# Scan readout in four column groups with four transfers a round, its products in banks of their own, rotary products one round later, nine lags

## The chip, the cores and the metric

The kernel runs on one core of one Trainium2 chip. The metric is the device time of one execution in microseconds (us): the kernel before takes 1859.64 us, the median of three runs (1855.35 to 1863.19). The engines are TensorE (PE in the rows; PEld is its weight load), VectorE (DVE), ScalarE (ACT), GpSimd (POOL) and SyncE (SP); ACT and SP also issue transfers (ACTq, SPq).

## What is computed

Two layers. Each projects its input (256 context and 256 latent tokens, width 1024) to a bidirectional state-space scan (S5), a grouped-query attention with rotary positions and a neighbourhood attention, gates and merges the three, and runs a mixture of 16 experts. The change is in the scan's readout and in the rotary step beside it:

```python
def apply_axial_rope(x, cos, sin):
    ...
    out = jnp.stack([x1 * cs - x2 * sn, x2 * cs + x1 * sn], axis=-2)
...
def s5_bidirectional(u_ctx, u_lat, lam_re, lam_im, log_dt, b_re, b_im, c_re, c_im, d_skip, need_ctx):
    ...
    def scan_direction(seq, d):
        lam_bar = jnp.exp(lam * dt)
        b_bar = ((lam_bar - 1.0) / lam)[..., None] * lax.complex(b_re[d].astype(f32), b_im[d].astype(f32))
        bu = jnp.einsum('blgh,gph->blgp', ug.astype(jnp.complex64), b_bar)
        _, states = lax.associative_scan(_recurrence_combine, (a, bu), axis=1)
    ...
    def readout(states, d):
        y = jnp.einsum('blgp,ghp->blgh', states, cm).real
    ...
    y_lat = (readout(st_f[:, n_ctx:], 0) + readout(st_b[:, :n_lat], 1)
             + dsk * u_lat.astype(f32)).astype(u_lat.dtype)
```

There are 32 groups of 16 channels with 64 complex states each, in two directions.

## The kernel before

**The scan in blocks of eight tokens.** The 512 tokens are 64 blocks of 8 steps. What a block takes from earlier blocks comes through its carried state `st`; what it takes from its own tokens comes through a 128 x 128 matrix per group (8 steps x 16 channels on either side), built from the products of `cre`, `cim` with powers of the transition (`pws`), here called lags. `cp` holds those products: 128 partitions (64 states of the forward direction, 64 of the backward), `NPOS` = 10 lag positions x 16 channels, for 4 groups, real and imaginary, two buffers.

**The loop around the change.** After the scan of the block states, each layer runs `for q in range(NQ + 1)`: 8 rounds of 4 groups and one round to finish. The loop is written once for each engine. In the order of the instructions, round q holds:

- TensorE: **z(q)**, 16 products that contract the 64 states of one direction (`bb`, 16 columns, stationary) with eight of the lags in `cp` (128 columns): the block matrix's entries, forward and backward in two PSUM banks, on partitions 0 to 15. **y(q-1)**, 24 products (128 x 64): `tm` by the input `ug`, and `cp` by the carried states `st`, into two banks. Then the four small products that turn a row of modulation weights into columns (`mc`), the sum of squares of a head's queries or keys (`qk_ms`, rounds 0 to 4), eight products of an input projection (rounds 0 to 4), eight column-tiled products of modulation weights (`mr`, 32 columns x 512), and in rounds 0 to 4 the **rotary product** of the same q, which waits for VectorE's normalised queries (`qnorm_done`). In rounds 5 to 8 of layer 0 an `mr` and an `mc` of the next layer come in as well. All of them are recorded at the helper's line L618; one fp32 product leaves two records.
- ScalarE: copies the forward bank of z into `zs` (L1132), waits for VectorE's part (`zd_done`), issues four of the eight transfers `zs` to `tm` (L1285), then the root of `qk_ms` (L1142) and the copies of projections and of modulation rows (`mrow`).
- VectorE: carries the block states (L1565 to L1568), copies and adds the backward bank of z and the skip weights into `zs` (`readout_rows`, L1528 to L1532), adds up y (L1815, L1817), the modulation block (L1737), for the last two rounds half of the `cp` products (`readout_part`, L1551 to L1553), the reciprocal and scaling of queries and keys (L1831, L1832), and the three rotary operations (L1837 to L1840).
- GpSimd: builds `cp` for a later round, six operations over 640 elements (L1992 to L2000), three in the rounds it shares with VectorE. Its buffer is one of two, so round q's starts when y(q-2) is complete.
- SyncE: the ring of weights from HBM (L535, 1 MB each) and the other four transfers to `tm` (L570), later the attention's bias (L540), which waits until the last y has been taken.

**Transfers to `tm`.** `zs` holds 16 rows and, for each group, 15 lags x 16 columns. Step j of the block matrix is a window of 128 columns that begins 16 columns further on, so one transfer for each j writes 16 partitions of `tm` for four groups.

**PSUM banks.** Nearly all products share four banks (`tile_ps`) that rotate by a list of jobs (`tile_jobs`); z and y take two each a round. A product waits until the bank it gets has been emptied. The banks `turn_ps` and `out_ps` are used elsewhere and idle in this loop.

## Time and profile before

| | us |
|---|---|
| median of three runs | 1859.64 |
| the profiled execution | 1862.84 |
| its span, first to last instruction | 1861.1 |
| TensorE busy | 1696.2 (91%) |
| VectorE / ScalarE / GpSimd busy | 704.6 / 417.7 / 302.4 |
| readout loop of layer 0, its stretch in the span | 177.3 to 314.3 |
| readout loop of layer 1 | 1241.3 to 1355.4 |

A view by stretches gives the busy time of each engine, the mean granted clock of TensorE (1.0 is its upper level, 2.4 GHz, 0.5 its lower, 1.2 GHz) and the share of time in which the transfer engines were busy. A timeline lists instructions in order of their start, with the idle time ahead of one and what ended it in square brackets. A table of waits sums up that idle time. The chain of work is followed back from the end, step by step, to what released each step.

### The profile page before, as it was taken

The numbers are of one execution on the slowest core, as the hardware profiler recorded it, in microseconds if no ns is written. First come the engines' busy times: TensorE is split into PE (matmuls) and PEld (weight loads), VectorE is DVE, ScalarE is ACT, GpSimd is POOL, SyncE is SP. The second block draws the span as 40 slices with busy tenths as digits, with TensorE's granted clock in tenths as the row PEclk, the third lists the DMA queues.
The fourth block names the chain that finished last, engine by engine and source line by source line (L and its number), as shares of the span: only waits on it lengthen the run. The fifth ranks groups of instructions, "written<-read, shape, count | busy, mean of one in ns | idle before, by whom it ended". The sixth has DMA issues, their size and how long they took to land.

```text
span 1861.1 us, 28871 instructions
## 1 busy us (share of the span) xinstructions
PE 1696.2 (91%) x11470; PEld 1028.1 (55%) x11470; DVE 704.6 (38%) x1564; ACT 417.7 (22%) x866; POOL 302.4 (16%) x263
## 2 busy tenths in 40 slices
PE   5999998889999999899988988999889999996697
PEld 2467455554444443555555556676547888453354
DVE  3678764650110112311101168596763111421123
ACT  4011212551000001322222250111144001331133
POOL 0004342870000000200000020045364000000000
PEclk9999998999999999999999988998999999998899
DMA  9410369419221153499999533125571346899991
GB/s 391 127 46 24 129 220 334 87 59 342 97 108 72 68 226 136 171 386 364 384 391 393 210 115 113 46 74 197 203 140 51 154 167 245 345 401 410 411 360 58
DMA packets 108139, 384.07 MB, mean 206 GB/s; under 512 B 42016, under 2 KB 61472, under 8 KB 68864
## 3 DMA queue, kind: packets, MB, share of 16 engines
q1 hardware_dynamic: 85872, 335.43, 48.2%
q0 software_dynamic: 4272, 30.67, 4.8%
q10 hardware_dynamic: 17888, 16.42, 3.1%
q8 instruction: 81, 1.33, 0.3%
q14 instruction: 26, 0.21, 0.0%
HBM read 363.09 MB, written 31.98 MB: 212 GB/s over the span
## 4 chain that ended last, share of the span: by engine, by line
PE 63%; DVE 12%; DMA 8%; SPq 7%; POOL 4%; issue 3%; ACT 3%; ACTq 1%; POOLq 0%; DVEq 0%
PE tile_ps L618 56%; SPq L535 6%; PE turn_ps L618 3%; DMA arena<-sorted_in 3%; POOL arena L2010 3%; DMA vn<-in_wpack 2%; PE out_ps L618 1%; DMA ring<-in_wpack 1%; PE turn_ps L939 1%; DVE arena L1873 1%; DMA arena<-in_rpb 1%; DMA x<-in_xT 1%; DVE arena L1518 1%; DVE arena L1565 1%; DVE arena L1516 0%
## 5 line engine op out<-in xcount | busy, mean ns | idle before, releaser
L618 PE MATMUL tile_ps<-h,ring 128*128 128x512 f32 (+1 forms) x1312 | 480.4, 522 | 7.1 <-ACT h L1149 5.0
L618 PEld LDWEIGHTS tile_ps<-h,ring 128*128 128x128 f32 x1312 | 255.2, 196 | 216.1 <-issue 199.6
L618 PE MATMUL tile_ps<-arena 128*32 128x256 f32 (+5 forms) x3152 | 271.7, 351 | 19.2 <-ACT arena L1374 4.9
L618 PE MATMUL tile_ps<-arena,ring 128*128 128x512 f32 (+1 forms) x704 | 235.3, 486 | 2.7 <-issue 2.7
L618 PEld LDWEIGHTS tile_ps<-arena 128*32 128x32 f32 (+4 forms) x3152 | 182.2, 140 | 77.5 <-issue 46.9
L618 PEld LDWEIGHTS tile_ps<-arena,ring 128*128 128x128 f32 x704 | 133.6, 190 | 96.6 <-issue 87.6
L2010 POOL TENSOR_SCALAR arena<-arena,smx 128x512 f32<-128x512 f32 (+1 forms) x96 | 128.5, 1358 | 64.0 <-DVE smx L1861 63.6
L618 PE MATMUL tile_ps<-ring,arena 128*32 128x256 f32 (+2 forms) x1008 | 93.9, 418 | 17.1 <-DMA ring<-in_wpack 12.4
L1347 ACT ACTIVATE arena<-tile_ps 128x512 f32<-128x512 f32 (+1 forms) x56 | 27.5, 491 | 347.3 <-PE tile_ps L618 347.3
L1894 DVE TENSOR_TENSOR arena<-tile_ps,arena 128x512 f32<-128x512 f32 (+1 forms) x32 | 17.8, 558 | 212.2 <-PE tile_ps L618 212.2
L1992 POOL TENSOR_TENSOR arena<-arena 128x640 f32<-128x640 f32 x16 | 22.1, 1380 | 353.4 <-PE tile_ps L618 353.3
L618 PEld LDWEIGHTS tile_ps<-ring,arena 128*32 128x32 f32 (+1 forms) x1008 | 49.1, 123 | 52.0 <-issue 34.1
L618 PE MATMUL tile_ps<-qn,arena 128*64 128x256 f32 (+1 forms) x272 | 65.2, 395 | 12.9 <-DMA vn<-in_wpack 12.9
L1712 DVE TENSOR_TENSOR arena<-tile_ps,arena 64x256 f32<-64x256 f32 x24 | 10.0, 417 | 175.6 <-ACT arena L1219 175.6
L1972 POOL TENSOR_SCALAR h<-h,amuls,mods 128x256 f32<-128x256 f32 x12 | 12.1, 1020 | 393.1 <-DVE h L1586 353.7
L618 PE MATMUL tile_ps<-ring,h 128*128 128x256 f32 (+1 forms) x384 | 72.0, 350 | 0.0
L1316 ACT ACTIVATE arena<-tile_ps,smx 128x512 f32<-128x512 f32 (+1 forms) x96 | 58.6, 616 | 57.9 <-DVE smx L1855 57.8
L939 PE MATMUL turn_ps<-con,arena 128*128 128x128 f32 x320 | 52.2, 288 | 19.0 <-DVE arena L1865 11.7
L618 PEld LDWEIGHTS tile_ps<-ring,h 128*128 128x128 f32 x384 | 64.2, 194 | 7.0
L618 PE MATMUL tile_ps<-qa,arena 128*64 128x256 f32 (+1 forms) x272 | 65.2, 395 | 0.0
L1855 DVE TENSOR_REDUCE smx<-tile_ps 128x1 f32<-128x512 f32 (+1 forms) x96 | 54.8, 598 | 26.4 <-PE tile_ps L618 25.1
L939 PEld LDWEIGHTS turn_ps<-con,arena 128*128 128x128 f32 x320 | 34.0, 142 | 54.8 <-issue 25.4
(316 smaller groups left out, 2274.6 us busy)
## 6 DMA issues: line engine op xcount, KB each, us to landing
ring<-in_wpack SPq DMA_DIRECT2D x176, 1024.0 KB, 7.6
arena<-in_wpack SPq DMA_DIRECT2D x64, 1024.0 KB, 16.5
h<-in_wpack SPq DMA_DIRECT2D x15, 1024.0 KB, 25.3
qa<-in_wpack SPq DMA_DIRECT2D x12, 1024.0 KB, 9.6
qn<-in_wpack SPq DMA_DIRECT2D x12, 1024.0 KB, 12.8
kn<-in_wpack SPq DMA_DIRECT2D x12, 1024.0 KB, 15.0
vn<-in_wpack SPq DMA_DIRECT2D x12, 1024.0 KB, 17.0
sorted_out<-arena ACTq DMA_DIRECT2D x44, 128.0 KB, 7.6
```

What stands on the lines that cost most here:

```text
L535: sp.dma_start(dst, src).then_inc(arrived, 16)
L618: return nc.tensor.matmul(out, lhsT, rhs, start=start, stop=stop)
L939: ins = nc.tensor.transpose(turn_ps[:, half, t * P:(t + 1) * P], probs[:, N % (LAG + 1), half, t * P:(t + 1) * P], c("ident"))
L1316: A(probs[:, N % (LAG + 1), half, 0:nk], bank((l, "sc", n, half))[:, 0:nk], ACT.Exp, bias=smx[:, 0, at:at + 1], accum_out=smx[:, 1, at:at ...
L1347: free(job, A(sig[:, n % 2, c0:], bank(job)[:, c0:], ACT.Sigmoid))
L1518: link(TT(nxt, nxt, tmp[0], ALU.add))
L1565: ins = TT(tmp[k], spread(came, 1, STEP), spread(pwb[:, k, 0:STEP, gs], 3, NB - 1), ALU.mult)
L1855: dve.tensor_reduce(smx[:, 0, at:at + 1], bank(job)[:, 0:nk], AX.X, ALU.max, negate=True).then_inc(max_done, 1)
L1873: link(TT(b, b, spread(c("far_cols"), 1, 2 * GRID_H), ALU.add))
L1894: free(job, TT(v, bank(job)[:, c0:], s, ALU.mult))
L1992: link(TT(o0, pv[0], cv[0], ALU.mult))
L2010: pool.tensor_scalar(v, v, smx[:, 2, at:at + 1], None, ALU.mult).then_inc(prob_done, 1)
```

## The change

- `NPOS` is 9 instead of 10: the forward lags are positions 0 to 7 for z and 1 to 8 for y, the backward ones 1 to 8 and 0 to 7, so both directions lie in nine positions. GpSimd's and VectorE's `cp` operations shrink from 640 to 576 elements.
- z's stationary matrix gets 32 columns (`bb_on`; the upper 16 are the next group's and their results aren't used). Group g of the round writes partitions 32g to 32g + 31 of `turn_ps`, forward in one bank and backward in another, so the products lie on eight tiles of 64 rows x 32 columns. `zs` is 128 partitions with 240 columns: the copies are 128 x 128 and 128 x 112 instead of 16 x 512 and 16 x 448.
- One transfer for each group, whose source is the overlapping windows of 16 rows (`lag_rows`), writes all 128 partitions of `tm`: four a round, two issued by SP and two by ACT, instead of eight. The order of `tm`'s rows changes from (step, channel) to (channel, step), and with it the input `ug`, `pww`, `wm` and the skip weights.
- y goes to `out_ps`. z and y have semaphores of their own (`z_full`, `z_free`, `y_full`, `y_free`) and no jobs in the rotation of `tile_ps`. Before the attention, TensorE waits for `y_free` and `z_free`, ScalarE ahead of its store of y for `y_free`.
- The rotary product of q - 1 moves into round q, behind `mc`; VectorE's three rotary operations move behind y's sum (and behind `readout_part`), in `rotated`.

```diff
-NPOS = STEP + 2
+NPOS = STEP + 1
...
-ON_SP = 4
+ON_SP = 2
...
-            names += [(l, "z", q, 0), (l, "z", q, 1)] if q < NQ else []
...
+            names += late
+            names += [(l, "rope", q - 1)] if 0 < q <= KW + 1 else []
...
-            names += [(l, "rope", q)] if q <= KW else []
...
+        def lag_rows(g):
+
+            v = zs[32 * g:32 * g + GRP, 0:P]
+            (step, n), (one, m) = v.ap
+            return bass.AP(tensor=v.tensor, offset=v.offset, ap=[[step, n], [GRP, STEP], [one, m]])
...
-                    for j in range(STEP - ON_SP, STEP):
-                        a = (STEP - 1 - j) * GRP
-                        sp.dma_start(tm[j * GRP:(j + 1) * GRP, q % 2], zs[:, :, a:a + P]).then_inc(tm_in, 16)
...
+                    for g in range(GQ - ON_SP, GQ):
+                        sp.dma_start(tm[:, q % 2, g], lag_rows(g)).then_inc(tm_in, 16)
+                sp.wait_ge(y_free, (l + 1) * NQ)
...
+                        if l * NQ + q:
+                            for n in range(2):
+                                pe.wait_ge(z_free[n], l * NQ + q)
+                        for r in range(2):
+                            for g in range(GQ):
...
+                                    ins = mm(turn_ps[32 * g:32 * g + 32, n, 0:P], bb_on[d, at_g:at_g + 32],
                                              cp[d, r, at_q, lags].rearrange("p a b -> p (a b)"), r == 0, r == 1)
...
+                    if 0 < q <= KW + 1:
+                        pe.wait_ge(qnorm_done, l * (KW + 1) + q)
+                        v = qa[:, q - 1, CTX:] if q - 1 < KW else ka[:, CTX:]
+                        product((l, "rope", q - 1), [(c("rot"), v)], bank((l, "rope", q - 1))[:, 0:LAT])
...
-                    if q <= KW:
-                        pe.wait_ge(qnorm_done, l * (KW + 1) + q + 1)
-                        v = qa[:, q, CTX:] if q < KW else ka[:, CTX:]
-                        product((l, "rope", q), [(c("rot"), v)], bank((l, "rope", q))[:, 0:LAT])
 
                 us = pairs[l]
+                for taken in (y_free, *z_free):
+                    pe.wait_ge(taken, (l + 1) * NQ)
...
-                link(CP(pww[F], pw[F, :, 0:STEP][:, :, ::-1]))
-                link(CP(pww[B], pw[B, :, 0:STEP]))
+                link(CP(pww[F], pw[F, :, 0:STEP].rearrange("p r j g -> p r g j")))
+                link(CP(pww[B], pw[B, :, 0:STEP][:, :, ::-1].rearrange("p r j g -> p r g j")))
...
+                    if 0 < q <= KW + 1:
+                        rotated(l, q - 1)
...
-                    if q >= 2:
-                        wait_full(pool, (l, "yb", q - 2))
-                        wait_full(pool, (l, "y", q - 2))
+                        pool.wait_ge(y_full, l * NQ + q - 1)
```

TensorE in rounds 0 and 1 of layer 0, before: `arena 16x128` are z's products, `arena 128x64` y's, `con,mrow` is `mc`, `qsq,con` is `qk_ms`, `h,ring` the projection, `ring,csil` is `mr`, `qa,con` the rotary product.

```order
L618 MATMUL tile_ps<-ring,csil 32x512 x8
L618 MATMUL tile_ps<-qa,con 128x256
L618 MATMUL tile_ps<-arena 16x128 x16
L618 MATMUL tile_ps<-arena 128x64 x24
L618 MATMUL tile_ps<-con,mrow 128x2 x4
L618 MATMUL tile_ps<-qsq,con 128x512
L618 MATMUL tile_ps<-h,ring 128x512 x8
L618 MATMUL tile_ps<-ring,csil 32x512 x8
L618 MATMUL tile_ps<-qa,con 128x256
```

The same place now:

```order
L623 MATMUL tile_ps<-ring,csil 32x512 x8
L623 MATMUL turn_ps<-arena 32x128 x16
L623 MATMUL out_ps<-arena 128x64 x24
L623 MATMUL tile_ps<-con,mrow 128x2 x4
L623 MATMUL tile_ps<-qa,con 128x256
L623 MATMUL tile_ps<-qsq,con 128x512
L623 MATMUL tile_ps<-h,ring 128x512 x8
L623 MATMUL tile_ps<-ring,csil 32x512 x8
```

The rotary product left the end of the round, where it stood right behind VectorE's scaling, for the middle of the next one; z and y write other banks.

VectorE in one round of layer 1, before, from the scaling of queries to the next one (L1565 to L1568 carry the states, L1528 to L1532 are `readout_rows`):

```order
L1832 SCALAR_TENSOR_TENSOR qa<-qa,qg,rstd 128x256
L1837 TENSOR_TENSOR qrt<-tile_ps,con 128x256
L1838 TENSOR_TENSOR qa<-qa,con 128x256
L1840 TENSOR_TENSOR qa<-qa,qrt 128x256
L1565 TENSOR_TENSOR arena<-arena 128x224 x2
...
L1528 COPY arena<-tile_ps 16x4x112
L1530 TENSOR_TENSOR arena<-arena,tile_ps 16x4x16
L1532 TENSOR_TENSOR arena<-arena 16x4x16
L1815 COPY arena<-tile_ps 128x256
L1817 TENSOR_TENSOR arena<-arena,tile_ps 128x256
L1737 TENSOR_TENSOR mods<-tile_ps,mis 128x8
```

The same round now:

```order
L1848 SCALAR_TENSOR_TENSOR qa<-qa,qg,rstd 128x256
L1571 TENSOR_TENSOR arena<-arena 128x224 x2
...
L1534 COPY arena<-turn_ps 128x112
L1536 TENSOR_TENSOR arena<-arena,turn_ps 128x16
L1538 TENSOR_TENSOR arena<-arena 128x16
L1830 COPY arena<-out_ps 128x256
L1831 TENSOR_TENSOR arena<-arena,out_ps 128x256
L1754 TENSOR_TENSOR mods<-tile_ps,mis 128x8
L1744 TENSOR_TENSOR qrt<-tile_ps,con 128x256
L1745 TENSOR_TENSOR qa<-qa,con 128x256
L1747 TENSOR_TENSOR qa<-qa,qrt 128x256
```

The three rotary operations moved from ahead of the states' carry to behind y's sum.

SP's transfers in the first rounds of layer 0, before and then now:

```order
L570 DMA arena<-arena 16x4x128 x4
L535 DMA ring<-in_wpack 128x2048 x4
L570 DMA arena<-arena 16x4x128 x4
L535 DMA ring<-in_wpack 128x2048
L570 DMA arena<-arena 16x4x128 x4
```

```order
L576 DMA arena<-arena 128x1x128 x2
L542 DMA ring<-in_wpack 128x2048 x4
L576 DMA arena<-arena 128x1x128 x2
L542 DMA ring<-in_wpack 128x2048
L576 DMA arena<-arena 128x1x128 x2
```

Two transfers of 128 rows stand where four of 64 rows stood; the weights' place between them is the same.

## Rows read from the trace of the kernel before

**Rows 1.** Busy time (instructions), granted clock, transfer share, GB/s, by stretches of both loops.

```profile
core 0: us, PE busy (x) PEld busy (x) DVE busy (x) ACT busy (x) POOL busy (x), PEclk, DMA share, GB/s
177.30:199.00 21.70, 19.58 (x85) 8.69 (x84) 19.51 (x46) 5.83 (x9) 0.00 (x0) 0.98 0.45 156
199.00:267.60 68.60, 67.47 (x497) 37.67 (x496) 43.88 (x76) 11.17 (x19) 33.96 (x24) 0.96 0.39 126
267.60:314.30 46.70, 41.57 (x467) 26.94 (x466) 22.87 (x59) 6.01 (x11) 8.43 (x6) 0.93 0.97 375
...
1241.30:1260.10 18.80, 18.80 (x87) 8.63 (x88) 16.19 (x44) 5.04 (x9) 0.00 (x0) 1.00 0.40 130
1260.10:1319.10 59.00, 56.42 (x497) 40.90 (x496) 38.04 (x76) 9.57 (x20) 33.87 (x24) 0.88 0.51 170
1319.10:1355.40 36.30, 29.82 (x369) 22.45 (x370) 25.84 (x53) 3.48 (x6) 9.80 (x6) 0.90 0.79 283
```

**Rows 2.** TensorE's waits in the loop of layer 0: us, times, longest.

```profile
PE tile_ps L618 <- ACT mrow L1132: 4.2, 4, 1.8
PE tile_ps L618 <- DVE qa L1832: 2.1, 1, 2.1
PE tile_ps L618 <- DVE arena L1817: 1.3, 3, 0.6
```

**Rows 3.** TensorE's waits in the loop of layer 1.

```profile
PE tile_ps L618 <- DVE arena L1553: 3.8, 1, 3.8
PE tile_ps L618 <- POOL arena L1995: 1.9, 1, 1.9
```

**Rows 4.** Timeline of TensorE, layer 1: start, duration, records.

```profile
1241.37 1.92 PE L618 MATMUL tile_ps<-arena 64*16 64x128 f32 x32
...
1264.78 1.05 PE L618 MATMUL tile_ps<-con,mrow 128*128 128x2 f32 x8
1265.70 0.68 PE L618 MATMUL tile_ps<-qsq,con 128*128 128x256 f32 x2
1266.33 5.38 PE L618 MATMUL tile_ps<-h,ring 128*128 128x256 f32 x16
1271.64 1.92 PE L618 MATMUL tile_ps<-ring,csil 128*32 128x512 f32 x16
1273.50 0.70 PE L618 MATMUL tile_ps<-qa,con 128*128 128x256 f32 x2
1274.29 4.78 PE L618 MATMUL tile_ps<-arena 64*16 64x128 f32 x80
...
1311.45 3.69 PE L618 MATMUL tile_ps<-h,ring 128*128 128x256 f32 x16 [0.57 <-DVE arena L1817]
...
1352.59 3.04 PE L618 MATMUL tile_ps<-arena 64*128 64x64 f32 x48
```

**Rows 5.** Chain of work in layer 1, rounds 1 to 2: start, duration, what.

```profile
1264.93 0.42 issue
1265.36 1.34 POOL arena L1992
...
1272.70 1.55 POOL arena L2000
...
1274.29 13.94 PE tile_ps L618 x124
```

**Rows 6.** Timeline, layer 1, two stretches: the same VectorE operation beside GpSimd and alone.

```profile
1293.21 1.33 POOL L1992 TENSOR_TENSOR arena<-arena 128x640 f32<-128x640 f32 x1 [5.01 <-PE tile_ps L618]
1293.27 1.34 DVE L1532 TENSOR_TENSOR arena<-arena 16x64 f32<-16x64 f32 x1
...
1294.54 0.41 DVE L1815 COPY arena<-tile_ps 128x256 f32<-128x256 f32 x1
...
1334.40 0.21 DVE L1532 TENSOR_TENSOR arena<-arena 16x64 f32<-16x64 f32 x1
```

**Rows 7.** ACT's twelve transfers to `tm` in rounds 5 to 7 of layer 0.

```profile
DMA to landing us min/median/max: 3.2/4.3/5.1
```

More of the change, by code:

```diff
@@ L344, in backbone @@
         into = st[:, STEP]
-        pww, a0 = cut(a0, [2, STEP, NGRP])
+        pww, a0 = cut(a0, [2, NGRP, STEP])
         pws, a0 = cut(a0, [2, NPOS, NGRP])
@@ L867, in _ @@
                             pe.wait_ge(cp_other, l * len(SHARED) + SHARED.index(q) + 1)
-                        for n in range(2):
-                            wait_bank(pe, (l, "z", q, n))
-                        for g in range(GQ):
-                            at_q = (q % 2) * GQ + g
-                            for r in range(2):
-                                for n, (d, lags) in enumerate(((lower, slice(0, STEP)), (upper, slice(2, NPOS)))):
-                                    ins = mm(bank((l, "z", q, n))[0:GRP, g * P:(g + 1) * P], bb[d, r, q * GQ + g, :],
+                        if l * NQ + q:
[3 more added lines that the diff above has]
+                            for g in range(GQ):
+                                at_q, at_g = (q % 2) * GQ + g, (r * NGRP + q * GQ + g) * GRP
+                                for n, (d, lags) in enumerate(((lower, slice(0, STEP)), (upper, slice(1, NPOS)))):
+                                    ins = mm(turn_ps[32 * g:32 * g + 32, n, 0:P], bb_on[d, at_g:at_g + 32],
                                              cp[d, r, at_q, lags].rearrange("p a b -> p (a b)"), r == 0, r == 1)
                                     if (g, r) == (GQ - 1, 1):
-                                        full((l, "z", q, n), ins)
+                                        ins.then_inc(z_full[n], 1)
                     if q == NQ:
@@ L1276, in _ @@
                         if q:
-                            act.wait_ge(tm_in, 16 * STEP * (l * NQ + q))
-                        job = (l, "z", q, 0)
-                        copy(job, zs[:, :, (STEP - 1) * GRP:], bank(job)[0:GRP].rearrange("p (g n) -> p g n", g=GQ))
+                            act.wait_ge(tm_in, 16 * GQ * (l * NQ + q))
+                        act.wait_ge(z_full[0], l * NQ + q + 1)
+                        nc.scalar.copy(zs[:, (STEP - 1) * GRP:], turn_ps[:, 0, 0:P]).then_inc(z_free[0], 1)
                         act.wait_ge(zd_done, 2 * (l * NQ + q + 1))
                         if q >= 2:
-                            wait_full(act, (l, "y", q - 2))
-                        for j in range(STEP - ON_SP):
-                            a = (STEP - 1 - j) * GRP
-                            act.dma_start(tm[j * GRP:(j + 1) * GRP, q % 2], zs[:, :, a:a + P]).then_inc(tm_in, 16)
+                            act.wait_ge(y_full, l * NQ + q - 1)
+                        for g in range(GQ - ON_SP):
+                            act.dma_start(tm[:, q % 2, g], lag_rows(g)).then_inc(tm_in, 16)
                     if q == NQ:
@@ L1299, in _ @@
                         copy_rows(l, MOD1 + q)
-                for q in range(NQ):
-                    wait_taken(act, (l, "y", q))
-                    wait_taken(act, (l, "yb", q))
+                act.wait_ge(y_free, (l + 1) * NQ)
                 act.dma_start(y_dram.rearrange("j t (a g) c -> (j t a) g c", g=NGRP), ug).then_inc(y_out, 16)
@@ L1522, in readout_rows @@
                 if q:
[L1523 to L1525 removed]
+                    dve.wait_ge(tm_in, 16 * GQ * (l * NQ + q))
+                back = turn_ps[:, 1, 0:P]
                 mid = slice((STEP - 1) * GRP, STEP * GRP)
[L1527 to L1532 removed]
+                n = l * NQ + q + 1
+                dve.wait_ge(z_full[1], n)
+                CP(zs[:, 0:(STEP - 1) * GRP], back[:, 0:(STEP - 1) * GRP]).then_inc(zd_done, 1)
+                dve.wait_ge(z_free[0], n)
+                TT(zs[:, mid], zs[:, mid], back[:, mid], ALU.add).then_inc(z_free[1], 1)
+                dve.wait_ge(z_free[1], n)
+                TT(zs[:, mid], zs[:, mid], dsk[:, q, :], ALU.add).then_inc(zd_done, 1)
             def scan_blocks(l):
@@ L1730, in experts_on_chip, with rotated @@
                 dve.wait_ge(moe_done, l * NTOK // P * KD + KD)
+            def rotated(l, m):
+                v = qa[:, m, CTX:] if m < KW else ka[:, CTX:]
+                dve.wait_ge(qnorm_done, l * (KW + 1) + m + 1)
+                job = (l, "rope", m)
+                wait_full(dve, job)
+                free(job, TT(qrt[:], bank(job)[:, 0:LAT], c("sin"), ALU.mult))
+                link(TT(v, v, c("cos"), ALU.mult))
+                wait_taken(dve, job)
+                TT(v, v, qrt[:], ALU.add).then_inc(rope_done, 1)
             def modulation_block(l, n):
@@ L1777, in _ @@
                         wait_full(dve, (l, "wt", q - 1, 1))
-                    pv = [spread(pww[:, r, :, gs].rearrange("p j g -> p g j"), 3, GRP) for r in range(2)]
-                    bv = [spread(bb[:, r, gs, :], 2, STEP) for r in range(2)]
+                    pv = [spread(pww[:, r, gs], 2, GRP) for r in range(2)]
+                    bv = [spread(bb[:, r, gs, :], 3, STEP) for r in range(2)]
                     link(TT(wm[:, 0], pv[0], bv[0], ALU.mult))
@@ L1810, in _ @@
                         o = q - 1
[L1811 removed]
                         v = ug[:, o * GQ:(o + 1) * GQ].rearrange("p g c -> p (g c)")
[L1813 to L1817 removed]
+                        dve.wait_ge(y_full, l * NQ + o + 1)
+                        link(CP(v, out_ps[:, 1, 0:GQ * NCH]))
+                        TT(v, v, out_ps[:, 0, 0:GQ * NCH], ALU.add).then_inc(y_free, 1)
                     if 0 < q < NQ:
```

81 lines of the change are left out of this document (29 added, 52 removed).

## The prediction

> **What bounds the kernel now.** The sum is made on the profiled execution, 1862.84 us; it lies 3.2 us above the median of 1859.64, and the forecast is moved down by that. I read first the two readout loops by stretches [rows 1]: together they are 251 of 1861 us, and they have different limits.
>
> In rounds 0 to 4 of layer 0 (177.3 to 267.6) TensorE is busy 87.05 of 90.3 us, so what it is given less comes off almost whole. In rounds 5 to 8 (267.6 to 314.3) it is busy 41.57 of 46.7 us, but the transfer engines are busy 97% of the time at 375 GB/s: each round loads four blocks of weights of 1 MB, and a faster TensorE meets that stream. In layer 1 the first round is TensorE's alone (18.80 of 18.80). In rounds 1 to 4 (59.0 us) TensorE is still busy 56.42 us, at a mean granted clock of 0.88, while GpSimd has 33.87 us of work that can't spread over a round: it starts when y is complete and z of a later round waits for its end. The chain of work shows that [rows 5]: y's end, 0.42 us of hand-over, six GpSimd operations from 1265.36 to 1274.25, and z at 1274.29. In rounds 5 to 8 the waits are on the operations that VectorE and GpSimd share [rows 3], 3.8 and 1.9 us. The table of waits for layer 0 [rows 2] has 2.1 us on the scaling of queries that the rotary product of round 0 needs, 1.3 us on the sum of y (a projection waits for its bank; two of the three are 0.6), and 4.2 us on ScalarE's copies of modulation rows, the longest (1.8) while ScalarE is issuing its transfers.
>
> **The change, part by part.**
>
> *z in column groups.* z's 32 records take 1.92 us alone, and 1.74 inside the 4.78 that z and y take together, since y alone takes 3.04 [rows 4]. z has 128 moving columns a record on two row tiles: 4,096 record-columns. The modulation product works on four column tiles and moves 16 x 512 = 8,192 record-columns in the same 1.92 us [rows 4]. So the pace doubles from two tiles to four. If eight tiles double it again, z takes 0.48 us, and if the change reaches only four at a time, 0.96; if the tiles don't overlap further, nothing is gained. No eight-tile product stands in the trace. I take 0.48, because the step from two to four shows no loss: 1.3 us less for each of 16 z's, of which the stretch decides what reaches the end. The Trainium skill (TensorE: Matmul & The Clock Gate, section "Wait — 56ns, not 53.3ns?") speaks of a floor of about 25 ns from the start of one matmul to the next, however few its columns, by which 32 records would need an estimated 0.8 us; a round would then keep 0.3 us more than in my sum, and no row here has products on eight tiles to test it.
>
> *Rounds 0 to 4 of layer 0.* Round 0 loses the wait of 2.1 [rows 2], z's 1.3, and the rotary product of 0.7 [rows 4], which goes to the next round: -4.1. Each of rounds 1 to 4 keeps one rotary product and loses z's 1.3: -5.2. With z and y out of the rotation of banks, the two waits of 0.6 on y's sum go: -1.1. The rotary product moves behind `mc`, long after the scaling of the round before, so I cost its wait at nothing: what hides it is a whole projection. A sum of -10.4.
>
> *Rounds 5 to 8 of layer 0.* On TensorE there would be 3.9 less of z and up to 4.2 less of waits on ScalarE (which issues two transfers instead of four), 0.7 more of rotary product: up to -7.4. The transfers move the same bytes and are idle 3% of 46.7 us, which is 1.4. I take -2.5, near the transfers' end of 0 to -7.4, because each MB of weights stays.
>
> *Layer 1, round 0.* -1.3 for z and -0.7 for the rotary product: -2.0.
>
> *Layer 1, rounds 1 to 4.* GpSimd's round is 33.87/4 = 8.5 us; nine positions instead of ten make it 7.6, with 0.4 of gaps 8.0. Its chain is then z 0.48 + y 3.04 + hand-over 0.42 + 8.0 = 12.0 us. TensorE's round is 0.48 + 3.04 + 1.05 (`mc`) + 0.70 (rotary) + 0.68 + 3.69 + 1.92 = 11.6 us at the upper clock, 13.3 where the projection runs at the lower one (5.38 instead of 3.69, [rows 4]). VectorE has 38.04/4 = 9.5. Two limits so close, with one of them sometimes at half clock, I put at 12.5 a round: 50.0 instead of 59.0, -9.0. The bounds are 12.0 a round (-11.0) and 13.5 (-5.0, the rival below).
>
> *Layer 1, rounds 5 to 8.* z gives 1.3 in rounds 6 and 7, where it is on the path: -2.6. Of the 5.7 us of waits on the shared products [rows 3] I take off 3.5: these operations get a tenth shorter, and the three rotary operations and the rest of round 4's work no longer stand ahead of them on VectorE. -6.1, between -2.6 (no wait goes) and -8.3 (all go).
>
> *What is added.* Before the attention TensorE now waits until VectorE has emptied y. Two operations of 0.41 us like the copy in [rows 6] stand there; I take +1.0 for layer 1 (0 if the first wait of the softmax swallows it, 1.2 with the hand-over), and nothing in layer 0, where modulation products of the next layer follow y. The two `pww` copies write with a stride; by the same row they are some 0.4 each, and at worst double: 0 to +0.8 a layer, +0.4 taken, +0.8 in all. The transfers to `tm` keep their bytes, with twice the rows in each; ACT's land 3.2 to 5.1 us after issue in the busiest stretch [rows 7], a round is 12 us or more, so they are hidden. The order of `ug`'s rows changes a transfer that moves the same bytes: nothing, give or take a few tenths.
>
> **The sum:** -10.4 - 2.5 - 2.0 - 9.0 - 6.1 + 1.0 + 0.8 = -28.2 us. 1862.84 - 28.2 = 1834.6, and less 3.2, **1831 us**. Later stages begin when these loops end, so the gain carries through.
>
> **The rivals.**
>
> *Less comes through (1844).* Three things hold it back together. z overlaps only four at a time: 0.48 more for five z's of layer 0 and eight of layer 1, +6.2. Rounds 5 to 8 of layer 0 give nothing: +2.5. And VectorE and GpSimd get in each other's way: VectorE's 16 x 64 addition takes 1.34 us beside GpSimd's operation and ends when that does, against 0.21 alone [rows 6]. The rotary operations used to run while GpSimd waited for y; now they come after y's sum, in GpSimd's busy stretch. Two of them read two operands from SBUF. Each can wait for a whole GpSimd operation of 1.3 us and then make the next one wait 0.4, so rounds of layer 1 go from 12.5 to as much as 13.5: +4.0. Together -15.5. The Trainium skill (SBUF — State Buffer, Who interferes with whom) states just this exclusive lock for a VectorE instruction with two SBUF inputs; the row's 1.34 agrees.
>
> *More comes through (1820).* TensorE sets rounds 5 to 8 of layer 0 after all, because the weights were waiting for it (-4.9 beyond the forecast), layer 1's rounds come at GpSimd's 12.0 (-2.0), all shared waits go (-2.2), and the lower-clock stretches of layer 0 vanish: at a mean of 0.96 over 68.6 us [rows 1] some 5.5 us were at the lower level, which costs 2.7. Together -40.
>
> *It doesn't do what it says (1848).* The eight tiles don't overlap more than the two row tiles did: 13 z's keep 1.3, +17. Against it stands the pace of the modulation product [rows 4].
>
> *Slower: the transfers to `tm` land late.* One transfer now fills 128 rows from overlapping windows of 16, and two follow each other on a queue. They are issued some 3 us into a round and y needs them in the next, so about 10 us are free in layer 1 and 12.4 in layer 0. Above that TensorE waits in every round. The landing now is 5.1 at most [rows 7]. From 13.5 us on (8 x 3.5 + 8 x 1.1 = 37) it would eat the gain of 28 and 9 more; at 14 us the time would be near 1876. For it speaks only that twice the rows stand in each transfer; against it, that the rows and bytes of a round are the same.
>
> **How the numbers follow.** The forecast gets 0.55, less 0.25, more 0.12, no overlap 0.05, late transfers 0.03. A range of 1817 to 1847 holds the first three with some room and leaves out the other two. Half a per cent, about what a measurement of this kernel tells from no change, is 9.3 us: faster is below 1850.3. Forecast, less and more lie there, and the most of no overlap; faster 0.91, same 0.06, slower 0.03.
>
> **What would show it.** In the changed profile z's records of a round should start within about half a microsecond, y behind them taking 3 us. In layer 1 GpSimd's six operations should take 1.2 to 1.4 us each, and z should follow the last of them; a round of 12 to 13 us. The wait on the scaling in round 0 and those on y's sum should be gone. Rounds 5 to 8 of layer 0 should stand at a transfer share near 1.0 with waits of TensorE on weights, and the stretch be 44 us or so. The forecast is wrong if TensorE waits for `tm`, if z's records keep 60 ns each, if VectorE becomes the engine that TensorE waits for in layer 1, or if more of the loops runs at the lower clock than now (0.88 to 1.00 by stretch, [rows 1]).

## The result, and the profile after

| | before | changed | ratio, 95% interval |
|---|---|---|---|
| 17 runs each, median, us | 1863.19 (1855.05 to 1872.05) | 1850.28 (1839.39 to 1861.62) | 0.9934, 0.9918 to 0.9951 |
| four runs of the changed kernel on another occasion | 1861.06 | 1846.75 | 0.9920, 0.9903 to 0.9938 |
| the profiled execution | 1862.84 | 1845.37 | |

The change saves 12.9 us at the median, where 28 was forecast; 1850.28 lies above the range (1817 to 1847). Part of the distance to the forecast of 1831 is the base: the kernel before has 1863.19 in 17 runs, 3.6 above the median of three that the forecast started from. The profiled execution, 1845.37, lies 4.9 below the median. Executions of one kernel differ by up to 1.2% in 17, and the time goes with the mean granted clock: of the changed kernel's, the quickest (1839.39) had 0.961 and the slowest (1861.62) 0.952. So single stretches of one profile are read below together with the lower-clock time in them.

The stretches that answer to [rows 1], in the same columns, for the changed kernel:

```profile
192.50:252.40 59.90, 59.90 (x500) 33.45 (x496) 48.56 (x84) 10.10 (x19) 31.27 (x24) 0.97 0.46 159
252.40:300.00 47.60, 42.15 (x472) 26.70 (x468) 18.10 (x53) 5.49 (x11) 7.70 (x6) 0.86 0.96 367
1225.90:1243.20 17.30, 16.91 (x85) 7.21 (x84) 16.23 (x46) 4.29 (x8) 0.00 (x0) 1.00 0.41 138
1243.20:1298.80 55.60, 51.64 (x500) 39.30 (x496) 43.79 (x78) 8.18 (x19) 31.34 (x24) 0.85 0.50 171
1298.80:1338.80 40.00, 30.38 (x374) 22.32 (x370) 22.89 (x53) 3.14 (x7) 8.87 (x6) 0.74 0.78 283
```

Put beside [rows 1], and beside a second profile of the changed kernel (the run c1 below). The table measures from the start of one z to the start of the next, so it differs from the cuts of the rows by up to 0.1 us:

| stretch | before | changed | second profile | forecast change | measured change |
|---|---|---|---|---|---|
| layer 0, round 0 | 21.7 | 17.9 | 17.9 | -4.1 | -3.8, -3.8 |
| layer 0, rounds 1 to 4 | 68.6 | 59.9 | 58.2 | -6.3 | -8.7, -10.4 |
| layer 0, rounds 5 to 8 | 46.7 | 47.6 | 44.9 | -2.5 | +0.9, -1.8 |
| layer 1, round 0 | 18.7 | 17.3 | 17.3 | -2.0 | -1.4, -1.4 |
| layer 1, rounds 1 to 4 | 59.1 | 55.6 | 59.0 | -9.0 | -3.5, -0.1 |
| layer 1, rounds 5 to 8, up to the attention | 36.3 | 40.0 | 39.8 | -5.1 | +3.7, +3.5 |
| both loops | 251.1 | 238.3 | 237.1 | -29.0 | -12.8, -14.0 |

The forecast's other +0.8 lies ahead of the loops. Layer 0's first rounds gave what was forecast and more. The gap is almost all in layer 1. TensorE's waits there, to be read against [rows 3]:

```profile
PE out_ps L623 <- issue: 6.3, 2, 5.1
PE turn_ps L623 <- POOL arena L2007: 2.8, 2, 1.6
PE turn_ps L623 <- POOL arena L2002: 1.7, 1, 1.7
PE tile_ps L623 <- DVE arena L1831: 1.0, 1, 1.0
```

`out_ps` is y. It waits 6.3 us in two pieces for something the table can only call issue. TensorE's timeline of layer 1 shows the places (rounds 2, 4 and 5):

```profile
1255.54 0.67 PE L623 MATMUL turn_ps<-arena 64*32 64x128 f32 x32 [1.56 <-POOL arena L2007]
1256.15 4.75 PE L623 MATMUL out_ps<-arena 64*128 64x64 f32 x48
...
1285.01 3.06 PE L623 MATMUL out_ps<-arena 64*128 64x64 f32 x48 [1.20 <-issue]
...
1308.02 1.11 PE L623 MATMUL turn_ps<-arena 64*32 64x128 f32 x32 [1.72 <-POOL arena L2002]
1314.23 5.38 PE L623 MATMUL out_ps<-arena 64*128 64x64 f32 x48 [5.10 <-issue]
```

z now begins 0.61 us ahead of y (1255.54 to 1256.15), and y alone takes 2.93 at the upper clock. But y at 1314.23 stands 5.10 us idle ahead and then takes 5.38, the duration at the lower clock. What y waits for besides z's banks are the transfers to `tm` and the carried states. The rows of SyncE's queue at that place:

```profile
1298.05 3.66 SPq L542 DMA_DIRECT2D ring<-in_wpack  x4
1301.80 1.20 SPq L576 DMA_DIRECT2D arena<-arena  x2
```

Four weight loads of 1 MB, a burst, are issued from 1298.05 on, and SyncE's transfers to `tm` follow at 1301.80. For SP's and ACT's transfers of rounds 3 to 5 the trace has these times from issue to landing, where [rows 7] had 3.2 to 5.1:

```profile
DMA to landing us min/median/max: 2.4/8.7/11.7
...
DMA to landing us min/median/max: 2.6/8.5/11.3
```

The last of them, issued at 1302.4, lands 11.7 us later, at 1314.1; y starts at 1314.23. Before the change, a burst of four loads and the transfers behind it lay further apart (round 3 of layer 1), since VectorE had the rotary step of the round before to do ahead of its part of z:

```profile
1286.75 2.02 SPq L535 DMA_DIRECT2D ring<-in_wpack  x4
1294.64 3.25 SPq L570 DMA_DIRECT2D arena<-arena  x4
```

There they were issued 6.4 us after z's start in that round; now it is 1.9 to 2.6 us in the rounds of layer 1 that have a burst ahead, and 1.5 in layer 0.

The earlier issue alone is no loss, though: in both kernels the last transfer lands when the burst has. In round 5 of layer 0 the fourth load lands 12.9 us after z's start before the change and 14.0 after it, and the last transfer 14.5 us after z's start in both. What moved is y. That round took 15.3 us before and takes 12.3 now, so TensorE could begin y at 12.9 us and waits:

```profile
PE out_ps L623 <- issue: 1.7, 1, 1.7
```

So the theory: the rounds became shorter than the time in which a burst and the transfers behind it land, and TensorE waits for the transfers. A stretch at the lower clock lies around the wait of round 5 in layer 1; it sets in ahead of it, since z at 1308.02 already takes 1.11 us.

### The profile page after: what moved, and what is told of

It reads as the page before. It is cut to its first block, busy times and chain, and to the rows that moved or that the text cites. A ratio compares the mean times of both kernels' runs of the same rounds, so it can differ in the third digit from the quotient of the medians.

```text
span 1843.6 us, 28760 instructions
## 1 busy us (share of the span) xinstructions
PE 1677.1 (91%) x11470; PEld 1017.1 (55%) x11470; DVE 703.8 (38%) x1564; ACT 412.7 (22%) x866; POOL 293.1 (16%) x263
## 3 DMA queue, kind: packets, MB, share of 16 engines
q8 instruction: 81, 1.33, 0.3%
## 4 chain that ended last, share of the span: by engine, by line
PE 66%; DMA 9%; DVE 8%; SPq 7%; POOL 4%; issue 3%; ACT 2%; ACTq 0%; POOLq 0%; DVEq 0%
PE tile_ps L623 56%; SPq L542 6%; PE out_ps L623 4%; PE turn_ps L623 4%; DMA arena<-sorted_in 4%; POOL arena L2017 3%; DMA vn<-in_wpack 2%; DMA ring<-in_wpack 2%; PE turn_ps L948 1%; DVE arena L1881 1%; DMA arena<-in_rpb 1%; DMA x<-in_xT 1%; PE tile_ps L842 0%; DVE smx L1863 0%; ACT h L1395 0%
## 5 line engine op out<-in xcount | busy, mean ns | idle before, releaser
L623 PE MATMUL tile_ps<-arena 128*32 128x256 f32 (+3 forms) x1872 | 192.9, 398 | 15.3 <-ACT arena L1380 4.9
L623 PEld LDWEIGHTS tile_ps<-arena 128*32 128x32 f32 (+2 forms) x1872 | 110.4, 131 | 57.7 <-issue 33.5
L1902 DVE TENSOR_TENSOR arena<-tile_ps,arena 128x512 f32<-128x512 f32 (+1 forms) x32 | 17.9, 558 | 212.1 <-PE tile_ps L623 212.1
L623 PE MATMUL out_ps<-arena 64*128 64x64 f32 (+1 forms) x968 | 83.1, 328 | 8.0 <-issue 8.0
L623 PEld LDWEIGHTS out_ps<-arena 64*128 64x128 f32 (+1 forms) x968 | 69.1, 209 | 11.9 <-issue 11.9
L1999 POOL TENSOR_TENSOR arena<-arena 128x576 f32<-128x576 f32 x16 | 20.2, 1264 | 345.6 <-PE tile_ps L623 212.2
L1980 POOL TENSOR_SCALAR h<-h,amuls,mods 128x256 f32<-128x256 f32 x12 | 12.1, 1014 | 389.8 <-DVE h L1592 353.2
L623 PE MATMUL turn_ps<-arena 64*32 64x128 f32 (+2 forms) x904 | 63.1, 330 | 9.1 <-POOL arena L2007 2.8
## 6 DMA issues: line engine op xcount, KB each, us to landing
qn<-in_wpack SPq DMA_DIRECT2D x12, 1024.0 KB, 12.2
kn<-in_wpack SPq DMA_DIRECT2D x12, 1024.0 KB, 14.6
```

Source lines behind the costliest of these rows:

```text
L623: return nc.tensor.matmul(out, lhsT, rhs, start=start, stop=stop)
L1902: free(job, TT(v, bank(job)[:, c0:], s, ALU.mult))
L1980: pool.tensor_scalar(v, v, amuls[:, nn // 2, which, k, 1:2], mods[:, nn // 2, 3 * which, k, 1:2], ALU.mult, ALU.add).then_inc(h_odd, 1)
L1999: link(TT(o0, pv[0], cv[0], ALU.mult))
```

## The experiments

### e1: the transfers ahead of the burst

```diff
-                    at = next_slots(min(used + RING, n_static))
+                    to = min(used + RING, n_static)
+                    at = next_slots(to if q in (0, NQ) else min(to, at + 1))
...
+                    at = next_slots(to)
```

> In each round after the first, SyncE issues one weight load, then the transfers to tm, then the remaining weight loads of the round; nothing else differs from the changed kernel. Theory of the burst (the transfers land late because they are now issued 1 to 3 us behind four loads of 1 MB): TensorE's waits of 1.7 us (layer 0, round 5), 1.2 and 5.1 us (layer 1, rounds 4 and 5) on tm go, the transfers land 3 to 6 us after issue in place of 8 to 12, the last four rounds of layer 1 take 33 to 35 us in place of 40.0, and the time falls by 6 to 10 us to a ratio of about 0.988 to 0.990 to the kernel before. Theory of the form (transfers of 128 rows are slow themselves): they still land 8 to 12 us after issue, the ratio stays at 0.993. If the lower clock after the wait has another cause, the waits go but the ratio improves by only 3 to 4 us.

Measured: median 1848.52 us, ratio 0.9937 (0.9915 to 0.9958). SyncE's queue, and the landing of SP's and ACT's transfers in rounds 3 to 5 of layer 1:

```profile
1298.42 0.33 SPq L542 DMA_DIRECT2D ring<-in_wpack  x1
1304.96 1.19 SPq L577 DMA_DIRECT2D arena<-arena  x2
1306.20 2.66 SPq L542 DMA_DIRECT2D ring<-in_wpack  x4
```

```profile
DMA to landing us min/median/max: 2.3/2.5/3.4
...
DMA to landing us min/median/max: 2.7/3.3/5.4
```

The stretches of this run, rounds 5 to 8 of layer 0, rounds 1 to 4 and 5 to 8 of layer 1:

```profile
255.00:306.50 51.50, 43.52 (x470) 24.08 (x466) 18.28 (x53) 5.48 (x11) 7.69 (x6) 0.83 0.86 328
1251.60:1300.00 48.40, 45.45 (x501) 33.83 (x498) 42.09 (x71) 8.76 (x20) 31.43 (x24) 0.96 0.63 219
1300.00:1336.40 36.40, 30.18 (x372) 22.95 (x372) 24.11 (x56) 2.55 (x7) 8.47 (x6) 0.79 0.83 304
```

With the same form of transfer, landing falls to 2.3 to 5.4 us, so the queue ahead makes the difference. In round 5 they are even issued later than in the changed kernel, 5.0 us after z's start instead of 2.6. In layer 1 rounds 1 to 4 take 48.4 us (12.1 a round, at a clock of 0.96) instead of 55.6, and rounds 5 to 8 36.4 instead of 40.0, where 33 to 35 were expected. Yet the median is no better, and the expectation of 0.988 to 0.990 was missed. In layer 0 TensorE now waits for weights:

```profile
PE tile_ps L625 <- DMA ring<-in_wpack: 5.5, 5, 2.4
```

SyncE stands at the wait for `zd_done`, 56.5 us in layer 0's loop instead of 30.1. Rounds 5 to 8 of layer 0 went from 47.6 to 51.5, their transfer share from 0.96 to 0.86. Not all of these 3.9 us is the edit's: the same stretch takes 50.7 in e3, whose edit is in layer 1 alone, with 20.5 us at the lower clock, and 44.9 to 45.1 in three executions with 6.8. By 47.6 us at 13.7 of it (the changed kernel) and 50.7 at 20.5, a stretch with e1's 17.1 would take an estimated 49, so the order costs 2.5 us of the 51.5. In this profile both loops together are 7.0 us shorter than the changed kernel's, and 6.5 are lost in stretches that the edit doesn't touch; that the order in layer 0 costs time shows in the medians, by e5.

### e2: eight transfers of 64 rows at the same place

```diff
-                        sp.dma_start(tm[:, q % 2, g], lag_rows(g)).then_inc(tm_in, 16)
+                        for k in range(2):
+                            sp.dma_start(tm[k * NST:(k + 1) * NST, q % 2, g], lag_rows(g, k)).then_inc(tm_in, 16)
...
```

> Each transfer to tm is split into two of 64 rows, eight in a round again, at the same place in the queues as in the changed kernel. Theory of the burst: landing times of the last one stay at 10 to 12 us in rounds 3 and 5 of layer 1, TensorE's wait of about 5 us stays, the ratio to the kernel before stays within 0.992 to 0.996. Theory of the form: landing falls to 3 to 5 us, the wait goes, ratio 0.988 to 0.990.

Measured: 1855.31 us, ratio 0.9966 (0.9947 to 0.9985); the trace gives no landing times here. TensorE's waits in layer 1:

```profile
PE out_ps L625 <- issue: 8.9, 3, 6.0
PE turn_ps L625 <- POOL arena L2010: 2.8, 2, 1.6
```

The wait on `tm` stays, 6.0 us at the longest, as the theory of the burst has it; the ratio lies just above its 0.992 to 0.996. The number and height of the transfers isn't the cause of the wait; if anything, four are better than eight.

### e3: products in TensorE's waits for GpSimd

```diff
...
+                        if l in (1,) and q >= 2:
+                            for k in range(2):
+                                mm(turn_ps[:, 0, P:512], c("ident"), con[:, 0:384])
...
```

The wait for z's banks moves ahead of these products.

> In layer 1, ahead of z in rounds 2 to 7, TensorE runs two products whose result nobody reads (128 x 128 by 384 columns, about 1.3 us in all), in the time in which it waits for GpSimd. Theory of the clock (TensorE's short waits for GpSimd are followed by stretches at the lower clock, which make TensorE the limit again): the granted clock of rounds 1 to 4 of layer 1 rises from 0.85 to 0.95 or more, those rounds take 50 to 52 us in place of 55.6, and the time falls by 3 to 6 us. Rival (the clock falls for other reasons): the clock stays near 0.85 and the rounds take 55 to 59 us, since the added work lies on the path in the slow rounds; the time rises by 1 to 4 us.

Measured: 1845.03 us, ratio 0.9927 (0.9898 to 0.9956), not to be told from the changed kernel. Rounds 1 to 4 of layer 1:

```profile
1253.20:1304.30 51.10, 51.03 (x517) 36.69 (x513) 42.55 (x72) 8.76 (x20) 31.51 (x24) 0.97 0.56 191
```

51.1 us at a clock of 0.97, where the changed kernel has 55.6 at 0.85 (59.0 at 0.80 in its second profile). GpSimd's work is the same. With the waits filled, the clock stays up in this execution and the rounds are shorter in spite of 1.6 us more work ahead of each z. The wait on `tm` in round 5 (3.3 us) remains, and rounds 5 to 8 take 39.4. That the waits are what brings the lower clock doesn't follow from it: e9 below keeps the wait ahead of round 2 and keeps the clock.

### e4: the rotary product back in its own round

```diff
-            names += [(l, "rope", q - 1)] if 0 < q <= KW + 1 else []
...
+            names += [(l, "rope", q)] if q <= KW else []
...
-                        rotated(l, q - 1)
...
+                        rotated(l, q)
```

> The rotary product and its three VectorE operations go back to the end of their own round, as in the kernel before; all else as in the changed kernel. If the move is worth what the prediction gave it: round 0 of layer 0 gets its wait of 2.1 us back, rounds of layer 1 get a wait of 1 to 1.5 us where the scaling is late, and the time rises by 3 to 6 us (ratio 0.995 to 0.997). Rival of the lock (the moved operations, now beside GpSimd's, cost as much as they save): VectorE's busy time in rounds 1 to 4 of layer 1 falls from 43.8 to 38 to 40 us, the transfers to tm are issued later behind the weight loads and land sooner after issue, and the time is the same or lower.

Measured: 1850.94 us, ratio 0.9946 (0.9929 to 0.9962). Rounds 1 to 4 of layer 1:

```profile
1245.90:1299.30 53.40, 49.35 (x499) 36.57 (x498) 36.04 (x76) 8.10 (x20) 30.96 (x24) 0.90 0.52 178
```

Neither theory holds whole. Round 0 of layer 0 gets 0.6 us longer (18.5), the rotary product itself, but the wait of 2.1 us [rows 2] doesn't come back in this execution. The scaling is done 17.2 us after z's start here, 18.8 in both profiles of the changed kernel and 20.6 before the change, and the rotary product's turn comes at 17.9. Only 0.4 us of that is VectorE's shorter work on z (the copy and two additions); the rest is how far VectorE lags when the loop begins. So how much of the 2.1 us belongs to the move stays open: at 18.8 the product would have waited an estimated 0.9.

The transfers are issued 6.5 us after z's start again (rounds 2 to 5 of layer 0), and they land 4.9 to 7.2 us after issue in round 5 of either layer. But the last of them still lands 14.2 and 14.3 us after z's start there, behind the burst, and layer 1 keeps its waits on them, 1.1 us in round 4 and 3.2 in round 5:

```profile
PE out_ps L623 <- issue: 4.6, 3, 3.2
```

So it is the move of the rotary step that brought the issue forward, and it isn't the early issue that makes TensorE wait.

The lock is there: VectorE is busy 36.04 us instead of 43.79, and 6.3 of these 7.8 us are the two rotary operations with both operands in SBUF, which no longer run beside GpSimd. In the changed kernel they read

```profile
1248.69 1.32 DVE L1745 TENSOR_TENSOR qa<-qa,con 128x256 f32<-128x256 f32 x1
1250.05 1.51 DVE L1747 TENSOR_TENSOR qa<-qa,qrt 128x256 f32<-128x256 f32 x1
```

against 0.41 and 0.43 before the change. But VectorE had that time to spare, GpSimd's work is nearly the same (30.96 and 31.34 us), and the total of the move can't be told from nothing.

### e5: the transfers ahead in layer 1 alone

```diff
-                    at = next_slots(min(used + RING, n_static))
+                    to = min(used + RING, n_static)
+                    at = next_slots(to if l == 0 or q in (0, NQ) else min(to, at + 1))
...
+                    at = next_slots(to)
```

> Transfers to tm ahead of the rest of the weight burst in layer 1 alone; layer 0 stays as in the changed kernel. Theory of the burst with the weight stream as the limit of layer 0's end: rounds 1 to 4 of layer 1 take 48 to 50 us and rounds 5 to 8 about 36 (as in the run with both layers, 48.4 and 36.4), rounds 5 to 8 of layer 0 go back from 51.5 to 47 to 48; the time falls by 7 to 10 us against the changed kernel, ratio 0.988 to 0.990. Rival (what is saved in layer 1 is lost elsewhere, or was the chance of one execution): ratio 0.992 to 0.995.

Measured: **1839.52 us, ratio 0.9883 (0.9857 to 0.9909)**, faster than the kernel before, and by 7.2 us at the median than the changed kernel on the same occasion (c1, 0.9903 to 0.9938; the intervals touch). It differs from e1 in layer 0 alone, and the two intervals don't overlap: holding the queue there costs. The three stretches as for e1:

```profile
252.60:299.70 47.10, 41.88 (x470) 26.71 (x466) 18.08 (x53) 5.48 (x11) 7.68 (x6) 0.86 0.96 369
1240.20:1289.10 48.90, 45.50 (x500) 33.73 (x496) 43.29 (x75) 8.72 (x20) 31.45 (x24) 0.97 0.62 219
1289.10:1332.00 42.90, 37.72 (x372) 28.30 (x372) 24.16 (x56) 2.59 (x7) 8.47 (x6) 0.60 0.73 261
```

Layer 0 is back at 47.1, and rounds 1 to 4 of layer 1 keep 48.9. Rounds 5 to 8 took 42.9 in this execution, not 36, nearly all of it at the lower clock (mean 0.60), though y waits for nothing there: TensorE waits 2.7 us ahead of z in round 6 for the shared `cp` operations, and the lower clock sets in. So in these rounds the lower clock isn't tied to the wait on `tm`.

### e6: as e5, with products in the waits of rounds 6 and 7

```diff
...
+                        if l in (1,) and q >= 6:
+                            for k in range(3):
+                                mm(turn_ps[:, 0, P:512], c("ident"), con[:, 0:384])
...
```

> As the run before, and in layer 1 three products whose result nobody reads (about 1.9 us) ahead of z in rounds 6 and 7, where TensorE waits for the shared cp operations. Theory of the clock: rounds 5 to 8 of layer 1 go from about 36 us with some 15 us at the lower clock to 32 to 34 us with less than 7 us at it. Rival: the lower clock stays, and the rounds take 36 to 39 us.

Measured: 1841.56 us, ratio 0.9900 (0.9874 to 0.9926). Rounds 5 to 8 of layer 1:

```profile
1288.20:1326.00 37.80, 32.17 (x382) 22.44 (x382) 24.47 (x56) 2.55 (x6) 8.88 (x6) 0.87 0.82 297
```

37.8 us at 0.87: the rival's time (36 to 39), with about 10 us of lower clock, between the two expectations, instead of 34 in e5 and 15 in e1. It is no faster than e1's 36.4, since the filling takes time itself, and the ratio isn't better than e5's. It doesn't pay.

### e7: half of the weights for layer 0's last rounds

```diff
+                        if l == 0 and 30 <= n < 46:
+                            sp.dma_start(ring[:, n % RING, 0:1024], wpack[first + n][:, 0:1024]).then_inc(slot_in[n % RING], 16)
+                            continue
```

> Sixteen of the weight loads of layer 0, those issued from its round 4 on, bring half of their columns; TensorE takes the rest from what lay in the slot, so the weights are wrong and only rounds 5 to 8 of layer 0 are to be read. Theory that the weight stream limits those rounds: they fall from 47.6 us to 39 to 42, and the wait on tm (1.7 us) goes. Rival (TensorE's clock and ScalarE's copies limit them): 45 to 48 us with the transfer share near 0.6.

Measured for rounds 5 to 8 of layer 0, and beside it the same stretch of the second profile of the changed kernel:

```profile
254.80:296.50 41.70, 38.35 (x470) 23.85 (x466) 18.57 (x53) 5.48 (x11) 7.92 (x6) 0.92 0.72 222
```

```profile
253.20:298.10 44.90, 38.31 (x472) 24.41 (x468) 18.08 (x54) 5.48 (x11) 7.69 (x6) 0.92 1.00 383
```

At the same clock (0.92) and the same TensorE work the stretch is 3.2 us shorter, with no wait on `tm`; e6 and e9, at that clock with all weights, take 45.1 both. So at this clock the weight stream does limit it, at a transfer share of 1.00, but what lies behind is near: TensorE's 38.4 us and its waits on ScalarE's copies make about 41. At more of the lower clock the stretch is longer (47.6 with 13.7 us of it, 50.7 with 20.5 in e3), so the clock counts there as well.

### c1: the changed kernel once more

> The changed kernel once more, for a second profile: every theory expects a ratio of 0.993 and waits on tm in rounds 4 and 5 of layer 1 like the first (1.2 and 5.1 us). If the lower clock follows these waits, rounds 5 to 8 of layer 1 have 15 to 20 us of it again; if it comes by chance, the number differs.

Measured: ratio 0.9920 (0.9903 to 0.9938). The waits come back at the same places:

```profile
PE out_ps L623 <- issue: 7.4, 2, 5.7
PE turn_ps L623 <- POOL arena L2007: 2.8, 2, 1.6
PE turn_ps L623 <- POOL arena L2002: 1.7, 1, 1.7
```

They are not the chance of one execution. Rounds 5 to 8 of layer 1 have 16.4 us at the lower clock, the 15 to 20 of the theory, after 20.5 in the first profile; but without the long wait on `tm` there are 15.3, 33.9 and 16.9 in e1, e5 and e9, so the theory isn't borne out. In rounds 1 to 4 of layer 1 the lower clock differs by run: 17.1 and 23.9 us in the two profiles of the changed kernel, 23.9 in e2 and 20.5 in e7, which leave the order in layer 1 as it is, 10.2 in e4, and 3.4 in each of e1, e3, e5, e6 and e9, which either move the transfers or fill the waits. The kernel before has 13.7 there.

### e8: the same edit on the kernel before

```diff
-                    at = next_slots(min(used + RING, n_static))
+                    to = min(used + RING, n_static)
+                    at = next_slots(to if l == 0 or q in (0, NQ) else min(to, at + 1))
...
+                    at = next_slots(to)
```

> The kernel before, with the same edit as the run e5: in layer 1 one weight load, then the transfers to tm, then the rest of the round's loads. Theory that the late transfers are a wait that the change itself made: in the kernel before they are issued 5 to 6 us into a round, after the burst has mostly landed, and TensorE waits for none; the edit brings nothing, ratio 0.997 to 1.003 (weights may come late: up to 1.003). Rival (the order of SyncE's queue was worth 10 us before the change as well): ratio 0.993 to 0.996.

Measured: 1866.85 us, ratio 1.0010 (0.9989 to 1.0032). Before the change the order of the queue was worth nothing, give or take the interval. That is the net: the table of waits for layer 1 now has 4.3 us on weights, and neither in it nor in the table of the kernel before does y wait for `tm`. The wait for late transfers is one that the change made.

### e9: two loads ahead, in layer 1 and in round 5 of layer 0

```diff
...
+                    at = next_slots(to if q in (0, NQ) or (l == 0 and q != 5) else min(to, at + 2))
...
```

> The changed kernel with two weight loads ahead of the transfers to tm, then the rest, in layer 1 and in round 5 of layer 0. Theory of the burst: two loads take some 5 us, so the transfers land 5 to 8 us after issue, still before y needs them; TensorE has no wait of over 1 us on tm nor on the weights of round 1 of layer 1 (1.7 us in the run e5); ratio 0.986 to 0.990. Rival (the transfers must be ahead of all but one): waits of 2 to 4 us on tm in rounds 4 and 5 of layer 1 come back, ratio 0.991 to 0.994.

Measured: 1840.99 us, ratio 0.9887 (0.9861 to 0.9913), as good as e5. Rounds 1 to 4 and 5 to 8 of layer 1:

```profile
1243.00:1291.80 48.80, 45.31 (x507) 33.97 (x506) 42.08 (x71) 8.76 (x20) 31.44 (x24) 0.97 0.57 197
1291.80:1329.70 37.90, 30.74 (x370) 23.52 (x370) 24.08 (x56) 2.55 (x6) 8.47 (x6) 0.78 0.83 297
```

TensorE's wait on `tm` is 0.9 us at the longest. Weights are waited for 2.7 us once, in layer 0. In rounds 3 to 5 of layer 1 the transfers land 2.3 to 5.5 us after issue, sooner than the 5 to 8 expected: the loads ahead were issued 5.1 us and more before them.

This run also settles something on the clock. Ahead of round 2 of layer 1 it has the very wait of the changed kernel, 1.56 us for GpSimd, and y behind it runs at the upper clock:

```profile
1255.39 0.67 PE L625 MATMUL turn_ps<-arena 64*32 64x128 f32 x32 [1.56 <-POOL arena L2009]
1255.99 2.93 PE L625 MATMUL out_ps<-arena 64*128 64x64 f32 x48
```

In both profiles of the changed kernel 10.2 us at the lower clock follow that wait. So the wait alone doesn't bring it, and what else does is open.

## Why the prediction was wrong

**z in column groups: right.** z takes 0.6 us to the start of y, where 0.48 was forecast and 0.96 was the lower case. Its 32 records start in four groups of eight, 6 to 11 ns apart in a group, so eight tiles do run at once. By the floor that the prediction cited from the Trainium skill (TensorE: Matmul & The Clock Gate, section "Wait — 56ns, not 53.3ns?") z would have needed an estimated 0.8 us. The 0.6 measured is less, so that floor doesn't hold across eight tiles here, and it doesn't explain the 0.12 us over the sum.

**Rounds 0 to 4 of layer 0: right, and undersized.** -10.4 forecast, -12.5 and -14.2 measured. At the upper clock a round takes 14.6 us instead of 16.8, so it saves 2.2 where 1.6 were forecast, the wait on y's sum included.

**"So they are hidden", of the transfers to `tm`: the step that failed.** It took the landing of [rows 7], 5.1 us at most, as a property of the transfer, and set it against the length of a round. In these runs landing is set by the burst of weight loads ahead. Those rows are from transfers issued 3.4 to 6.4 us into a round, when half of the burst had landed. Now they are issued 1.5 to 2.6 us into a round, stand behind the whole 4 MB and take 7 to 12 us, and the last lands 13.8 to 15.4 us into the round, much as before the change (14.5 in round 5 of layer 0 and round 3 of layer 1). The rounds became shorter than that, so y waits: 1.7 us in layer 0 and 1.2 and 5.1 in layer 1, 8.0 together. e1, e5 and e9 change the queue ahead, and the waits of layer 1 go; e4 changes the time of issue, and waits stay. The last rival named late landing, but gave it the wrong cause (twice the rows in each transfer; e1 and e2 refute it), counted 10 us of room from an issue at 3 us, and gave it 0.03.

**Rounds 1 to 4 of layer 1: the mechanism was right, its condition was missing.** 12.5 us a round were forecast; 13.9 and 14.8 came. GpSimd's chain is 12.0 to 12.4 us in the rounds at full clock (its operations take 1.22 to 1.47 us instead of 1.33 to 1.55, a tenth less, as forecast), and in e1, e5 and e9 the rounds take 12.1 to 12.2: 48.4 to 48.9 us, the forecast's 50.0 and a little better. What the prediction lacked is the clock. It knew 13.3 us as TensorE's work in a round whose projection runs at the lower clock, and took 12.5 as if the stretches stayed as short as before. In the changed kernel TensorE waits ahead of rounds 2 and 4, 7 to 14 us at the lower clock follow, and these rounds take 15.6 to 19.0. Two of the signs of being wrong that the prediction gave came, TensorE's waits for `tm` and more of the lower clock: both loops have 54.7 and 47.1 us at the lower clock in the two profiles, 34.5 before. Why the lower clock comes isn't shown. It is short with filled waits (e3) and with another order of the transfers (e1, e5, e9), but e9 has the wait ahead of round 2 unchanged.

**Rounds 5 to 8 of layer 1: wrong by 9 us.** -5.1 forecast, +3.7 and +3.5 measured. 5.1 to 5.7 of that is the wait on `tm`. Without that wait the stretch still takes 36.4, 42.9 and 37.9 us in e1, e5 and e9, against 36.3 before: TensorE still waits for the shared operations, and the stretch runs at a mean clock of 0.60 to 0.79 there, against 0.90 before. The prediction took 3.5 of 5.7 us of waits off and let nothing return. Why the lower clock lasts longer here than before isn't settled; in the one execution profiled, filled waits shorten it (e6) and cost what they bring.

**Rounds 5 to 8 of layer 0: size off.** The bound of the transfers in the prediction's own row was -1.4, and -2.5 was taken; +0.9 and -1.8 came. e7 shows the weight stream as the limit at the clock of the second profile (0.92); the first has 13.7 us at the lower clock there, 6.9 more.

**What was added** came as said: y's wait ahead of the attention is 0.97 us (1.0 forecast), and the two `pww` copies of layer 1 take 0.64 and 0.67 us instead of 0.42 each (+0.4 a layer forecast). The lock between VectorE and GpSimd is real in the rows (VectorE +5.8 us of busy time in rounds 1 to 4, and -7.8 in e4). The Trainium skill's page SBUF — State Buffer, section Who interferes with whom, states it for a VectorE operation with two SBUF inputs, and the trace agrees (1.32 and 1.51 us beside GpSimd, 0.41 and 0.43 without). It costs GpSimd little: its operations take 7.8 us a round with it and 7.7 without (e4), where 7.6 was forecast. On TensorE no cost can be measured.

Of the missing 15 us, taking the late transfers away in layer 1 brings back 7 us against the changed kernel on the same occasion (ratio 0.9920 to 0.9883), 9 against its 17 runs (0.9934): about half, by experiment. The waits on `tm` in layer 1 are 6.3 us; how the rest of that gain and the lower clock of rounds 1 to 4 hang together is open. What is still missing stands, by the stretches, in the last rounds of both layers.

## What to carry to other kernels

When a change shortens a round, don't carry a landing time over as so many us after issue. Look up what is queued ahead of the transfer and when that has landed, and set this against the time at which the consumer will now ask. Here the last transfers landed 14 to 15 us into a round before and after, and only the round got shorter. Where one queue has bulk loads and small urgent transfers, let one or two bulk loads go first, then the urgent ones, then the rest (e5, e9), but not throughout a stretch where the bulk stream is the limit (e1).

## What was not expected of the hardware

- The transfers that ACT issues were as late behind the burst of weight loads (8.5 us in the median) as those that SP issues behind its own loads (8.7).
- In rounds with four loads of 1 MB ahead, the last transfer landed 0.5 to 1.6 us after the last load, whether it was issued 6.4 us after z's start (before the change, rounds 3 and 5 of layer 0 and 3 of layer 1) or 1.5 to 2.6 (after it).
- Rounds 1 to 4 of layer 1 took 48 to 59 us in the changed kernel and its variants, with 3.4 to 23.9 us at the lower clock. The same wait of 1.56 us ahead of round 2 was followed by 10.2 us at the lower clock in two profiles and by the upper clock in a third (e9).
- Eight tiles of 64 x 32 start 32 records of 128 columns within 0.6 us, about 19 ns a record, against 60 on two row tiles of 64 rows [rows 4].
